# Running the attention projection's first row tile between the turns of the other tiles, and moving two modulation products

## What is computed

```python
for layer in range(2):
    mp = split(silu(c_ctx) @ mod_w[layer] + mod_b[layer], 6)      # six vectors of 1024, context
    ms = split(silu(c) @ mod_w[layer] + mod_b[layer], 6)          # and latent
    h = rmsnorm(x, norm1_g[layer]) * (1 + m[1]) + m[0]
    y = recurrent_mixer(h) if layer == 0 else attention(h)        # layer 1: q, k, v = h @ at_w_qkv, QK-norm, rotary,
                                                                  # banded window + cached context, then @ at_w_o
    x = x + m[2] * y
    x = x + m[5] * expert_choice_moe(rmsnorm(x, norm2_g[layer]) * (1 + m[4]) + m[3])   # 16 experts, F = 1024
```

## Time and profile before

| | |
|---|---|
| median of 3 runs | 1841.49 us (1841.22 to 1842.8) |
| profiled execution, its own time | 1842.19 us |
| its span | 1840.4 us |
| granted PE clock, mean | 0.95 |
| PE busy | 1667.6 us (91%) |
| PEld busy | 773.6 us (42%) |
| DVE busy | 596.8 us (32%) |
| ACT busy | 370.0 us (20%) |
| POOL busy | 306.1 us (17%) |
| moved by DMA | 524.99 MB, mean 285 GB/s |
| DMA rate in most slices of the expert stretches | 389 to 416 GB/s |

### The profile page before, as it was taken

The page is one execution under the profiler, slowest core; times in us unless marked ns, Lnnn a source line. Parts: engine busy times, 40 slices in busy tenths (PEclk is TensorE's granted clock), DMA queues, the critical chain, the costliest instruction groups (busy, mean ns, idle before and its releaser), DMA issues.

```text
span 1840.4 us, 30762 instructions
## 1 busy us (share of the span) xinstructions
PE 1667.6 (91%) x13341; PEld 773.6 (42%) x13341; DVE 596.8 (32%) x1159; ACT 370.0 (20%) x772; POOL 306.1 (17%) x395
## 2 busy tenths in 40 slices
PE   4999789599999999999979788894999999999997
PEld 1888466123333333332358666572233333333322
DVE  4387565311011011111366577455111210210102
ACT  3477722000000000000241366311000000000000
POOL 1134200100110110111011288201101101111110
PEclk8999989799999999999989899896999999999999
DMA  9411634999999999999720201226899999999982
GB/s 354 143 69 47 262 138 189 415 379 392 390 409 409 404 403 406 412 405 357 308 76 1 97 24 47 115 92 253 338 396 389 407 409 395 409 414 398 407 337 114
DMA packets 57934, 524.99 MB, mean 285 GB/s; under 512 B 12607, under 2 KB 12895, under 8 KB 25038
## 3 DMA queue, kind: packets, MB, share of 16 engines
q1 hardware_dynamic: 48096, 490.62, 65.8%
q0 software_dynamic: 8176, 27.08, 5.3%
q10 hardware_dynamic: 1534, 5.38, 0.7%
HBM read 500.50 MB, written 22.55 MB: 284 GB/s over the span
## 4 chain that ended last, share of the span: by engine, by line
PE 80%; DVE 8%; ACT 5%; DMA 4%; issue 2%; POOL 1%; SPq 0%; DVEq 0%; ACTq 0%; POOLq 0%
PE ps L954 36%; PE ps L958 18%; PE ps L1212 5%; PE ps L872 4%; DMA W<-x_hat,gi_c 2%; PE ps L882 2%; PE ps L1234 1%; PE ps L1247 1%; PE ps L1260 1%; DMA ring<-in_mod_w 1%; PE ps L776 1%; PE ps L981 1%; PE ps L1097 1%; PE ps L1119 1%; PE ps L1099 1%
## 5 line engine op out<-in xcount | busy, mean ns | idle before, releaser
L954 PE MATMUL ps<-ring,W 128*32 128x512 f32 x4608 | 557.2, 601 | 4.0 <-issue 2.6
L958 PE MATMUL ps<-ring,W 128*16 128x512 f32 x2304 | 301.6, 595 | 0.0
L954 PEld LDWEIGHTS ps<-ring,W 128*32 128x32 f32 x4608 | 146.6, 111 | 337.7 <-issue 335.5
L1283 ACT ACTIVATE W<-ps 128x512 f32<-128x512 f32 (+5 forms) x137 | 72.0, 542 | 908.9 <-PE ps L996 707.7
L1799 DVE TENSOR_TENSOR W<-ps,amod 128x1024 f32<-128x1024 f32 (+1 forms) x32 | 28.5, 891 | 487.1 <-PE ps L981 364.6
L954 PE MATMUL ps<-over_rows,W 128*32 128x512 f32 x1536 | 182.7, 593 | 0.0
L958 PEld LDWEIGHTS ps<-ring,W 128*16 128x16 f32 x2304 | 67.9, 98 | 179.5 <-issue 179.5
L1808 DVE TENSOR_TENSOR W<-ps,W 128x1024 f32<-128x1024 f32 x16 | 19.6, 1225 | 277.5 <-PE ps L958 277.5
L958 PE MATMUL ps<-over_rows,W 128*16 128x512 f32 x768 | 99.9, 592 | 0.0
L954 PEld LDWEIGHTS ps<-over_rows,W 128*32 128x32 f32 x1536 | 48.1, 110 | 108.3 <-issue 107.8
L625 POOL DMA_INDIRECT x_mid<-W,si_l x14 | 20.1, 1434 | 367.1 <-DVE W L1819 303.3
(11 more groups left out here) (288 smaller groups left out, 2226.4 us busy)
## 6 DMA issues: line engine op xcount, KB each, us to landing
ring<-in_moe_w_down SPq DMA_DIRECT2D x52, 2048.0 KB, 11.7
ring<-in_moe_w_up SPq DMA_DIRECT2D x48, 2048.0 KB, 13.4
ring<-in_moe_w_gate SPq DMA_DIRECT2D x44, 2048.0 KB, 11.4
ring<-in_mod_w SPq DMA_DIRECT2D x48, 1024.0 KB, 8.1
over_rows<-in_moe_w_gate SPq DMA_DIRECT2D x20, 2048.0 KB, 11.2
over_rows<-in_moe_w_up SPq DMA_DIRECT2D x16, 2048.0 KB, 12.0
over_rows<-in_moe_w_down SPq DMA_DIRECT2D x12, 2048.0 KB, 12.9
ring<-in_rg_w_in SPq DMA_DIRECT2D x8, 1024.0 KB, 19.2
```

The lines of the kernel that those rows point to most:

```text
L954: nc.tensor.matmul(ps[q * CG:(q + 1) * CG, bank + n, :], lat(q, k), expert_slots(slots[q // 2], 1)[:, 0, cols], start=(k == 0), stop=(k == ...
L958: mm = nc.tensor.matmul(ps[q * CG:q * CG + CC, bank + 2, :], ctx(a, k), expert_slots(slots[a], 1)[:, 0, h * D + n * 512:h * D + (n + 1) * ...
L1283: nc.scalar.activation(out, in_, ACT.Copy).then_inc(done, n)
```

## The change

- Layer 0's last expert pair gets vector 9's product between its second and third slot pair.
- Vector 10's product runs after the sums' product of tile 3; vector 8's, whose weights are now loaded after the projection, runs in attention's third unit, in PSUM bank 4 with its turn in bank 7 and its row in ring slot 3.
- The projection's weight rows are used in their natural order; rows 0 to 3 are loaded behind vector 9's weights into slots 0 to 3 and cast by ACT, rows 4 to 7 after vector 10's product into slots 4 to 7 and cast by POOL. DVE takes rests 0 to 2 before the sums, rest 3 to 7 between the norms and turned rows of the later tiles.
- PE starts the projection's tile 0 when tile 0 is turned, and turns tiles 1 to 4 after its second, fourth, sixth and eighth weight row. The turn of the cached keys goes into tile 1.
- `new_k` and `new_v` are stored from ACT's queue after the last query turn; SP goes on to the loads of vector 8 and `at_w_o` as soon as the projection's matmuls are done.
- In `mixer_out`, layer 0 turns tile 0 between main terms and rests of tile 2; layer 1 no longer has tile 1's main terms before tile 0's rests.

The diff, cut to its core:

```diff
-MOD_SLOT = {..., 9: 8, 10: 0, 8: 0, 11: 8}
+MOD_SLOT = {..., 9: 8, 10: 4, 8: 4, 11: 8}
...
-QKV_ORDER = (4, 5, 6, 7, 0, 1, 2, 3)
+QKV_ORDER = tuple(range(KB))
...
-            return {2: 0, 3: 1, 4: 0, 5: 3, 11: 0}.get(n, 6)
+            return {2: 0, 3: 1, 4: 0, 5: 3, 10: 4, 11: 0}.get(n, 6)
+        def mod_turn_bank(n):
+            return 7 if n == 10 else 2
...
 (SP)
-            load_mod(10, moe_used, lambda s: LAYER_USES - 4 + s // 2 + 1)
-            for s in range(4, KB):
+            for s in range(4):
                 sp.wait_ge(moe_used, LAYER_USES - 4 + s // 2 + 1)
                 load_qkv(s)
-            load_mod(8, ring_used, lambda s: used(10, s))
-            for s in range(4):
-                sp.wait_ge(ring_used, used(8, s))
+            load_mod(10, moe_used, lambda s: LAYER_USES - 4 + (s + 4) // 2 + 1)
+            for s in range(4, KB):
+                sp.wait_ge(ring_used, used(10, s))
                 load_qkv(s)
-            sp.wait_ge(qn_ok, NT)
-            sp.dma_start(new_k, qn[:, NH * HD:NQK * HD]).then_inc(kv_stored, 16)
-            sp.wait_ge(v_ok, NT)
-            sp.dma_start(new_v, v_s[:, TL, :]).then_inc(kv_stored, 16)
             sp.wait_ge(qkv_mm, NT)
+            load_mod(8, None, None)
             for s in range(4):
                 put(KB + s, at_w_o[s])
...
 (POOL)
             experts(0)
+            mod_bias(8)
+            def qkv_high(k):
+                pool.wait_ge(wq_hi_ok, 2 * KB // 2)
+                pool.wait_ge(slot_ready[k], ready("qkv", k))
+                nc.gpsimd.tensor_copy(wq_hi[:, k, :], ring[:, k, 0:D]).then_inc(wq_hi_ok, 1)
+                nc.gpsimd.tensor_copy(wq[:, k, QKV:QKV + 512], ring[:, k, D:QKV]).then_inc(wq_hi_ok, 1)
+            qkv_high(4)
             pool.wait_ge(add_mm, NT)
...
-            for v in range(8, 11):
-                mod_bias(v)
+            for k in range(5, KB):
+                qkv_high(k)
+            mod_bias(9)
...
+                if u == 4:
+                    mod_bias(10)
...
 (PE, mixer_out)
-                    if t == 0:
-                        for u in range(2):
-                            main_terms(layer, u, first=(u == 0))
-                        weight_rests(layer, 0, first=True)
-                    elif t == 1:
-                        weight_rests(layer, 1, first=False)
-                    else:
-                        main_terms(layer, t, first=False)
-                        weight_rests(layer, t, first=False)
+                    if layer == 0 and t == 0:
+                        main_terms(layer, 0, first=True)
+                        main_terms(layer, 1, first=False)
+                    elif layer or t >= 2:
+                        main_terms(layer, t, first=(t == 0))
+                    if layer == 0 and t == 2:
+                        turn_rows(1, 0, xh_tile[0], (4, 5))
+                    weight_rests(layer, t, first=(t == 0))
                     if t == 0:
                         after_first()
-                    else:
-                        if t == 1:
-                            pe.wait_ge(gate_ok, 4 * (layer + 1))
+                    if t == 1:
+                        pe.wait_ge(gate_ok, 4 * (layer + 1))
+                    if t >= 2 or (layer and t == 1):
                         turn_rows(2 * layer + 1, t - 1, xh_tile[(t - 1) % 2], (4, 5))
...
 (PE, experts: last down product)
+                        if s == 1 and not more and layer == 0:
+                            modulation(8, turn_last=False)
...
-            modulation(8, turn_last=False)
-            modulation(9, turn_last=False)
             def between_rows(t):
-                if t >= 3:
-                    turn_x(t - 3)
+                if t == 0:
+                    turn_waiting()
+                if t == 3:
+                    modulation(9, turn_last=False)
+                    pe.wait_ge(mod_row, 10)
+                    turn_x(0)
+                if t == TL:
+                    turn_waiting()
             last_rows(0, between_rows)
-            modulation(10, turn_last=False)
-            for t in range(2, NT):
-                turn_x(t)
-            modulation()
-            turn_k(0, 6)
...
-            pe.wait_ge(mod_read, 11)
-            pe.wait_ge(row_act, 2 * NT)
-            pe.wait_ge(row_dve, 2 * NT)
+            pe.wait_ge(mod_read, 10)
+            pe.wait_ge(x2_ok, 2 * TL)
...
+                    if t == 0 and m % 2:
+                        turn_x(m // 2 + 1)
+                    if m == 1 and t == 1:
+                        pe.wait_ge(row_act, 2 * NT)
+                        pe.wait_ge(row_dve, 2 * NT)
+                        turn_k(0, 6)
...
 (PE, attention units)
+                if i == 2:
+                    modulation(10, turn_last=False)
+                if i == 3:
+                    turn_waiting()
...
+                    if u == 1:
+                        pe.wait_ge(mod_read, 11)
...
 (ACT)
+            mod_reads([8], turn_last=False)
+            for k in range(4):
+                qkv_high(k)
...
+            for t in range(NT):
+                square(t)
+                if t >= 1:
+                    row_root(2, t - 1)
+                if t == 0:
+                    row_waiting()
+                if t == 2:
+                    mod_reads([9], turns=False, turn_last=False)
+                if t == 3:
+                    turned(0)
+                    input_high(0)
+                    row_waiting()
+            row_root(2, TL)
+            turned(1)
+            input_high(1)
+            for t in range(2, NT):
+                turned(t)
...
             turned_q(NT - 1)
+            act.wait_ge(qn_ok, NT)
+            act.dma_start(new_k, qn[:, NH * HD:NQK * HD]).then_inc(kv_stored, 16)
+            act.wait_ge(v_ok, NT)
+            act.dma_start(new_v, v_s[:, TL, :]).then_inc(kv_stored, 16)
...
+                if i == 2:
+                    mod_reads([10], turn_last=False)
+                if i == 3:
+                    row_waiting()
...
 (DVE)
             norm_inputs(2, 1)
+            qkv_rest(range(3))
...
             def normed(t):
-                if 2 <= t < NT + 2:
-                    row_scale(2, t - 2, tok(r2)[:, t - 2, :], tok(w_xhat)[:, t - 2, :])
-                if 1 <= t <= NT:
+                if t >= 2:
+                    scaled(t - 2)
+                if t >= 1:
                     row_var_of(2, t - 1)
-                if t >= 3:
-                    rows_turned(2, 1, t - 3, feat(r1)[:, :, (t - 3) * P:(t - 2) * P], 7)
+                if t == 3:
+                    turned(0)
+                    input_rest(0)
             last_rows(0, normed)
-            for t in range(NT, NT + 3):
-                normed(t)
+            qkv_rest([3])
+            scaled(3)
+            row_var_of(2, TL)
+            qkv_rest([4])
+            turned(1)
+            scaled(TL)
+            qkv_rest([5, 6])
+            turned(2)
+            input_rest(1)
+            qkv_rest([7])
+            turned(3)
+            turned(TL)
...
-            input_rest(0)
-            qkv_rest(QKV_ORDER)
```

More of the change, by code:

```diff
@@ L748, in _, with turn_waiting, turn_row @@
             behind = []
-            def modulation(*vectors, turns=True, turn_last=True):
-                def turn_row(v):
-                    pe.wait_ge(mod_row, v + 1)
-                    if v == 8:
-                        pe.wait_ge(ob_ok, 41)
-                    if v:
-                        pe.wait_ge(mod_read, v)
-                    for j in range(4):
-                        mm = nc.tensor.transpose(ps[:, 2, j * P:(j + 1) * P], mod_rows(v)[:, j * P:(j + 1) * P], ident[:, :])
-                    mm.then_inc(mod_tr, 1)
+            def turn_waiting():
+                while behind:
+                    turn_row(behind.pop(0))
+            def turn_row(v):
+                pe.wait_ge(mod_row, v + 1)
+                if v == 8:
+                    pe.wait_ge(ob_ok, 41)
+                if v:
+                    pe.wait_ge(mod_read, v)
+                for j in range(4):
+                    mm = nc.tensor.transpose(ps[:, mod_turn_bank(v), j * P:(j + 1) * P], mod_rows(v)[:, j * P:(j + 1) * P], ident[:, :])
+                mm.then_inc(mod_tr, 1)
+            def modulation(*vectors, turns=True, turn_last=True):
                 for n in vectors:
                     v = MOD_ORDER[n]
-                    if n and n != 3:
+                    if n and n not in (3, 10):
                         pe.wait_ge(mod_row, n)
@@ L1513, in qkv_high, with row_waiting, input_high @@
                 copy(wq[:, k, QKV:QKV + 512], ring[:, k, D:QKV], wq_hi_ok)
-            mod_reads([8, 9], turn_last=False)
-            act.wait_ge(ring_used, used(9, 3))
+            def row_waiting():
+                turned_row(behind.pop(0))
+            def input_high(t):
+                if t >= 2:
+                    act.wait_ge(qkv_mm, t - 1)
+                act.wait_ge(row_act, row_at(2, t) + 1)
```

(8 more changed lines are left out.)

66 lines of the change are left out of this document (27 added, 39 removed).

## The result

| | before | changed |
|---|---|---|
| median | 1841.49 us (1838.17 to 1842.8, 5 runs) | 1831.2 us (1831.02 to 1834.23, 5 runs) |
| profiled execution, its span | 1842.19, 1840.4 us | 1831.02, 1829.2 us |
| granted PE clock, mean | 0.95 | 0.952 |
| PE busy | 1667.6 us | 1659.2 us |

The ratio is 0.9948 (95% interval 0.9935 to 0.996): 10.3 us faster by the medians, 11.2 by the two profiled executions. The forecast was 12.9 faster, 1828.6.

The account below looks back on a forecast made before the run. TensorE, 80% of the chain that ended last, was taken as the bound where it waits or runs at low clock. Terms -4.8 - 12.6 + 5.3 + 4.0 - 4.8 = -12.9 gave 1829.3, 1828.6 on the median's footing; range 1819 to 1837.

Parts of the forecast that it names:

- Part 1: Output projections: TensorE's 3.14 us stall before tile 0's turn and the low clock after it go, -4.8 us per layer.
- Part 2: Hand-over from layer 0's experts to the attention projection: projection starts at about 924.1 instead of 941.45, -12.6 us.
- The port: Hand-over: GpSimd's casts cost VectorE some slack beside its weight rests, taken as 1 us.
- My rival: Projection's first tile: each of eight GpSimd casts is added to VectorE's list, 5.7 us lost, 1833.3; chance 0.15.
- Part 3 (a): Start of attention: VectorE's first row maximum waits for the new_k and new_v stores, landing in 6.7 us, +5.3 us.
- Part 3 (b): Attention's third unit: vector 8's 32 matmuls delay the fourth scores and first transposes, and the delay stays, +4.0 us.
- (c): Attention: w_o lands about 22 us after the projection's end instead of about 20, before POOL asks; costs nothing.
- slower rival: Start of attention: stores land only when the loads ahead have (24.0 us), +22.6 us, 1845.9; chance 0.04.
- the interleave does nothing: Projection's tile 0: matmuls wait at each of four turns, its end stays at 959.8, 1841.2, no change; chance 0.05.

Follow-up runs that it names:

- e1: Kernel before with only the changed order of `mixer_out` in both layers: 1830.12 us, ratio 0.9931 to the kernel before.
- e3: Changed kernel with the high parts of weight rows 4 to 7 cast by ScalarE instead of GpSimd: 1830.18 us, ratio 0.994 to the kernel before.
- e2: Changed kernel with new_k and new_v stored from SP's queue between the loads of vector 8 and w_o: 1821.75 us, ratio 0.9893 to the kernel before.
- e8: Changed kernel with w_o's loads held until both stores have landed, stores still on ScalarE's queue: 1824.64 us, ratio 0.9915 to the kernel before.
- e5: Changed kernel with `mixer_out` put back to the order of before: 1842.93 us, ratio 1.0016 to the kernel before.

## Why the prediction came out as it did

The time lies in the forecast's range and 2.6 us above the forecast. But the sum came near by errors that cancel in part, so the nearness of the number is partly luck, and the steps show it.

- **Part 1 (-9.6).** The mechanism is right, and so is the size in the trace, -4.9 and -4.9. I left out what the stages behind take back, 1.2 and 0.4. e1 shows that the part stands alone, and gives it more, 11.5 by the medians, above my bounds of 6.6 to 10; its trace gives the projections 8.4 to 9 and the clock elsewhere 2.6. Tile 1's turn, costed at nothing, is on time.
- **Part 2 (-12.6).** Direction right, size 3.6 too high; -9.0 is within the bounds of -15 to -7. Its start: 27.1 us after the last expert matmul where I had 24.9. The mis-sized term is TensorE's product for tile 3's sums, "0.9": two such tiles take 6.02 us at the low clock, and VectorE stood 2.4 for them. Vector 10's product at 4.66 was too dear by 1.0, since that product had kept TensorE busy. (By its own terms, 18.3 and four turns of 0.87 from 924.1 on, my tile 0 ends at 945.9, not 945.7.)
- **The port.** I charged 1 us and put the casts beside the rests. They hit the scale of tile 2, which has one source and which I had not listed, for 3.5 us, and TensorE then waits at its turns (0.48 and 0.41 in the first trace, where it had run at the low clock before them, 2.72 in the second). e3 puts the price at 4.7 in A. My rival had 5.7 for it and was nearer in this term, and its total of 1833.3 is off by 2.1 where the forecast is off by 2.6.
- **Part 3 (a) (+5.3).** Mechanism right: the row maximum waits for `new_v`. The term was mis-sized: landing 6.7 by the scatter's row, 9.5 measured, +7.6; the 10.8 that I kept as the bound was nearer. e2 and e8 show why: w_o's loads in flight, not the queue.
- **Part 3 (b) (+4.0).** Too dear: +1.6 in the trace. At the second transposes, where I had laid out 3.5, it is 2.9. The term that I put at nothing is the clock behind the product: 1.1 comes back by the third transposes, because work that ran at the low clock before now runs at the full one. The 0.5 for GpSimd's bias does not show either. My step "from there each unit waits for the last, so it stays" held: the +1.7 of the third transposes is +1.6 at vector 11's product.
- **(c)** w_o at no cost: right in the changed kernel.
- Parts 2 and 3 together: forecast -3.3, ledger +0.3, e5 +2.2. Here the forecast was wrong in sign. In the profiled execution the two steps of the clock at the end of the ledger (3.3) covered it; by the medians it was Part 1, larger in e1 than forecast.
- The slower rival and "the interleave does nothing" are out: the stores landed in 9.5, not 24, and tile 0 of the projection holds the four turns in 24.1 us, with 0.9 of waits at them. But what the slower rival supposed is nearly what happened: `new_v` landed at 1039.2, after three of w_o's four loads and 1.5 before the last. Its price was wrong; its mechanism was near.
- The range: the lower bounds as given add up to 1817.4, not 1814. Nothing else hangs on it.

## What to carry to other kernels

An edit with several parts is worth measuring by parts: here one reordering of a few lines brought the whole gain, and what a long rework of the hand-over won (9.0) was eaten at attention's start by a wait for a store (7.6) and a product moved there (1.6). A small store on which an engine waits belonged here ahead of the large loads or between them, not behind them all: moving two stores of 128 KB ahead of 4 MB of loads was worth some 9 us. Casts on GpSimd are not free beside VectorE: ask which VectorE operation on SBUF, with one source or two, will stand next to a run of them. And take a second trace of the same kernel before a difference of 1 to 2 us is given to an edit.

## What the runs showed of the hardware

- A run of GpSimd casts holds one VectorE operation nearly to its end: 0.75 to 4.22 (single source), 1.2 to 3.88 (two sources); the first of the two came out the same in a second trace (4.23). An operation that reads PSUM was not stretched beside such a cast (1.37 at 918.19 beside 1.04 at 918.16), and with ScalarE casting the same rows the scales stayed at 0.75 and the wide rests at 1.21 to 1.23. Where casts and rests met singly, both were stretched (2.00 and 1.61).
- Stores of 128 KB land in 1.7 and 1.8 us with no load in flight (before) or only the last of vector 8's (e8), in 5.1 behind vector 8's and ahead of w_o's on one queue, in 7.1 and 9.5 with w_o's 4 MB issued before them.
- The four matmuls of a slot of a modulation product, into different partitions of one bank, run side by side: before, four start within 0.02 us (895.59 to 895.61) and the next four at 896.02. Alone they take as long: 8 take 4.88 us, 32 take 4.69 to 5.85 at the same place.
- Where TensorE takes up work after a wait, the same matmuls run at either level of the clock from one execution to the next (1.92 or 2.78 us, 1.93 or 3.51; the projection's first 6.2 us, behind a wait of 1.81, at a granted 0.51 or 1.00).
